# Differential attention beside an expert retrieval: other banks, other slots and a merged softmax in the attention steps

## The reference, cut to what matters

```python
def hybrid_mixer(x, ...):
    h = x @ w_in                                   # q, k, v, pooled input, gates
    q, k, v, p, g = split(h)
    a = softmax(q1 k1 * scale + bias) - lam * softmax(q2 k2 * scale + bias)   # 8 heads, causal, ALiBi
    o = rms_norm(a @ v, subln_g) * (1 - lam_init)
    attn_branch = o @ w_attn_proj
    pool_branch = (multiscale_pool(p) @ pool_w * pool_scale) @ w_pool_proj
    return (sigmoid(g_attn) * attn_branch + sigmoid(g_pool) * pool_branch) @ w_out
def peer_ffn(y, w_q, sub_keys, u, v):              # 8 heads, 16 experts each of 16384
    s = (y @ w_q) . sub_keys ; idx, gate = top-16 of the top-16 x top-16 sums, softmax
    act = gelu(u[idx] . y)
    return sum over 8 * 16 rows of gate * act * v[idx]
y = layer_norm(ALPHA * x + hybrid_mixer(x));  out = layer_norm(ALPHA * y + peer_ffn(y))
```

## Time and profile before

| what | value |
|---|---|
| time, median of 3 runs | 3320.99 us (3320.77 to 3330.28) |
| the profiled execution, its own time | 3328.37 us |
| its span | 3326.4 us |
| PE busy | 2798.8 us (84%) |
| DVE busy | 2475.0 us (74%) |
| ACT busy | 1162.4 us (35%) |
| POOL busy | 1324.7 us (40%) |
| DMA | 1244.97 MB, 374 GB/s over the span; the gathers are 1073.81 MB of it |

### The profile page before, as it was taken

The page is one execution under the profiler, slowest core; times in us unless marked ns, Lnnn a source line. Parts: engine busy times, 40 slices in busy tenths (PEclk is TensorE's granted clock), DMA queues, the critical chain, the costliest instruction groups (busy, mean ns, idle before and its releaser), DMA issues.

```text
span 3326.4 us, 30256 instructions
## 1 busy us (share of the span) xinstructions
PE 2798.8 (84%) x8368; PEld 1442.0 (43%) x8368; DVE 2475.0 (74%) x5989; ACT 1162.4 (35%) x3421; POOL 1324.7 (40%) x1248
## 2 busy tenths in 40 slices
PE   9999999999976799889988989867877777777776
PEld 7776565445433345444444544323433222222222
DVE  2316788896888778997799877888788676667664
ACT  2202555453122233445454522232323333333332
POOL 1101354554334343444454544344444444444432
PEclk9999999999998999999999999889989999999999
DMA  5635999999999999999999999999999999999997
GB/s 190 245 136 199 383 388 373 383 362 368 419 399 407 421 420 407 405 361 332 336 370 370 364 420 420 375 388 420 420 420 418 421 416 421 416 414 417 420 415 311
DMA packets 205223, 1244.97 MB, mean 374 GB/s; under 512 B 23680, under 2 KB 36992, under 8 KB 73600
## 3 DMA queue, kind: packets, MB, share of 16 engines
q0 software_dynamic: 147456, 1073.81, 79.8%
q1 hardware_dynamic: 56592, 169.11, 13.6%
q10 hardware_dynamic: 1008, 0.14, 0.0%
HBM read 1228.81 MB, written 14.16 MB: 374 GB/s over the span
## 4 chain that ended last, share of the span: by engine, by line
PE 41%; DMA 30%; DVE 18%; issue 6%; ACT 4%; POOL 1%; SPq 0%; POOLq 0%; DVEq 0%; ACTq 0%
DMA ring<-uv,idx 30%; PE r_o L1579 15%; PE w_ps L1373 14%; DVE ring L1306 8%; DVE z_e L1258 3%; PE w_ps L1421 2%; PE r_o L1550 1%; PE w_ps L1550 1%; PE w_ps L1516 1%; PE w_ps L1458 1%; PE w_ps L1493 1%; DVE e L1022 1%; POOL ring L706 1%; PE r_o L1493 1%; PE r_o L1516 1%
## 5 line engine op out<-in xcount | busy, mean ns | idle before, releaser
L706 POOL DMA_INDIRECT ring<-uv,idx x1024 | 1172.3, 1145 | 1722.9 <-PE r_o L1579 1231.0
L1579 PE MATMUL r_o<-ring,diag 128*128 128x512 f32 x2936 | 1445.6, 626 | 403.9 <-ACT diag L892 388.1
L1306 DVE CUSTOM_DVE_ANT_0 ring<-ring,ytok 128x1024 f32<-128x1024 f32 x768 | 937.1, 1221 | 234.1 <-DMA ring<-uv,idx 232.7
L1579 PEld LDWEIGHTS r_o<-ring,diag 128*128 128x128 f32 x2936 | 539.7, 195 | 1131.9 <-ACT diag L892 590.0
L879 ACT ACTIVATE gel<-dot 128x2 f32<-128x2 f32 x512 | 104.0, 203 | 1608.9 <-DVE dot L1306 1605.3
L1373 PE MATMUL w_ps<-x,w 128*128 128x384 f32 (+1 forms) x2112 | 655.4, 456 | 9.7 <-DMA x<-xT 5.9
L1373 PEld LDWEIGHTS w_ps<-x,w 128*128 128x128 f32 x2112 | 395.9, 192 | 230.0 <-issue 59.1
L1306 DVE CUSTOM_DVE_ANT_0 ring<-ring,zn 128x1024 f32<-128x1024 f32 x256 | 313.3, 1224 | 211.3 <-DMA ring<-uv,idx 211.3
L1258 DVE SCALAR_TENSOR_TENSOR z_e<-ring,coef,z_e 128x1024 f32<-128x1024 f32 x290 | 371.7, 1282 | 0.2 <-ACT coef L883 0.2
L892 ACT ACTIVATE diag<-ident,coef 128x128 f32<-128x128 f32 x734 | 262.8, 387 | 0.0
L883 ACT ACTIVATE coef<-gel,gate 128x1 f32<-128x1 f32 x1024 | 246.0, 287 | 16.8
(11 more groups left out here) (199 smaller groups left out, 2331.3 us busy)
## 6 DMA issues: line engine op xcount, KB each, us to landing
w<-w_in SPq DMA_DIRECT2D x132, 512.0 KB, 3.6
wq<-wq SPq DMA_DIRECT2D x46, 512.0 KB
wc<-w_branch SPq DMA_DIRECT2D x24, 768.0 KB, 8.4
ring<-uv,idx POOLq DMA_INDIRECT x1024
wo<-w_out SPq DMA_DIRECT2D x24, 512.0 KB, 10.7
xs<-x SPq DMA_DIRECT2D x8, 512.0 KB
out<-yn_e SPq DMA_DIRECT2D x8, 512.0 KB, 11.6
x<-xT SPq DMA_DIRECT2D x16, 192.0 KB, 4.0
```

The source lines that it names most:

```text
L706: nc.gpsimd.indirect_dma_start(out=ring[t % RING][:], out_offset=None, in_=a["uv"], in_offset=bass.IndirectOffsetOnAxis(ap=idx[:, slot:slo ...
L1306: nc.vector.tensor_tensor_reduce(ring[r][:, 0:D], ring[r][:, 0:D], y_of(n)[:], 1.0, 0.0, ALU.mult, ALU.add, dot[:, slot:slot + 1]).then_in ...
L1579: ins = nc.tensor.matmul(o_ps[n % 2][half][:], diag[(u - 1) % DIAGS][:], ring[t % RING][:, D + half * HALF:D + (half + 1) * HALF], start=s ...
```

## The change

* The values product (L1458) and the output turn (L1473) of groups 2 and 3 go to the two idle row-sum banks whenever their slot lies in 14 to 117 of a tile (from slot 78 on). Of group 3's 24 steps 20 lend the values' bank and 20 the output's; of group 2's steps 8 and 9. For these, the waits between output turns and scores, and between turns and `osb`, are gone; a tile's first sum waits for the last user.
* Group 3's step keeps its 7 slots, but its second chunk comes 3 slots after the first, and exponents, mix, turns, values and output come 1 to 3 slots later in it. Group 2's mix and what follows come 1 slot later. Everything behind group 3's attention comes 3 slots later, its scores too, so that VectorE adds 2 more rows.
* The mix is now e2 * ratio + e1 with ratio = -lambda * den1 / den2; the pass over the second softmax is gone. The first softmax's reciprocal is multiplied in where the values' product leaves PSUM (`osb`), for which the copy becomes a tensor_scalar.
* The exponent of the expert scores' softmax is put beside an attention exponent where one lies within 6 slots, and the copies of turned mixes stand ahead of exponents due in the same slot. `invert` and `share` come 4 slots later.

```diff
-DRAIN = (19, 23, 23)
+DRAIN = (19, 23, 26)
-DO_EXP = (3, 5, 5)
-DO_MIX = (5, 6, 6)
-DO_TURN = (8, 7, 7)
+DO_EXP = (3, 5, 6)
+DO_MIX = (5, 7, 8)
+DO_TURN = (8, 8, 10)
 TURN_LEN = (2, 2, 3)
-DO_ACROSS = (9, 8, 9)
-DO_VALUES = (11, 11, 13)
+DO_ACROSS = (9, 9, 11)
+DO_VALUES = (11, 12, 16)
-DO_OT = (22, 24, 25)
-BEHIND = (0, 4, 3)
+DO_OT = (22, 24, 27)
+SCORE_GAP = (2, 2, 3)
...
+def lent(slot):
+
+    return slot >= 78 and 14 <= slot % SLOTS < 118
...
+    def value_bank(g, k):
+        if values_lent(g, k):
+            return o_ps[((step_at(g, k) + DO_VALUES[g]) // SLOTS + 1) % 2][0]
         return o_ps[1][0] if g == 0 else ps[3]
...
+        def shares():
+            for g in range(1, RH * TT):
+                yield exponent_at(g)
+                exponent(g)
...
-                nc.vector.reciprocal(rden, den).then_inc(mix_step, 1)
-                dve.wait_ge(mix_step, 3 * m + 1)
-                nc.vector.tensor_scalar(c2, rden[:, 1:2], neglam, None, ALU.mult).then_inc(mix_step, 1)
-                dve.wait_ge(mix_step, 3 * m + 2)
-                nc.vector.tensor_scalar(both[:, 1, 0:n], both[:, 1, 0:n], c2, None, ALU.mult).then_inc(mix_step, 1)
-                dve.wait_ge(mix_step, 3 * m + 3)
+                nc.vector.reciprocal(rden[m % 4], den).then_inc(mix_step, 1)
+                dve.wait_ge(mix_step, 2 * m + 1)
+                nc.vector.tensor_scalar(ratio, rden[m % 4][:, 1:2], den[:, 0:1], neglam, ALU.mult,
+                                        ALU.mult).then_inc(mix_step, 1)
+                dve.wait_ge(mix_step, 2 * m + 2)
...
-                nc.vector.tensor_copy(osb_of(g, k)[:], value_bank(g)[:, 0:DV]).then_inc(o_copied, 1)
+                nc.vector.tensor_scalar(osb_of(g, k)[:], value_bank(g, k)[:, 0:DV], rden[m % 4][:, 0:1], None,
+                                        ALU.mult).then_inc(o_copied, 1)
...
-                    if c == 0 and g and k > BEHIND[g]:
-                        pe.wait_ge(o_ready, STEP0[g] + k - BEHIND[g])
+                    if c == 0 and output_behind(g, k):
+                        pe.wait_ge(o_ready, output_behind(g, k))
...
+                if output_lent(g, k):
+                    bank_free(step_at(g, k) + DO_OT[g])
+                elif g:
+                    pe.wait_ge(logit_done, scores_behind(g, k))
```

More of the change, by code:

```diff
@@ L86 @@
                (-23, -21, -8, -3, -1, 1, 3),
-               tuple(T_A[2] - 30 + 4 * i for i in range(7)))
+               tuple(T_A[2] - 32 + 4 * i for i in range(7)))
 LAST_UNITS = ((0, 2, 5, 7, 10, 12, 15, 17, 20),) + (tuple(range(0, 27, 3)),) * 2
-HEAD_UNITS = ((0, 3, 6, 9), (0, 3, 6, 11), (0, 5, 10, 16))
+HEAD_UNITS = ((0, 3, 6, 9), (0, 3, 6, 11), (0, 4, 8, 16))
 EARLY = T_A[0] + 30
@@ L124, in evacuated_at @@
 def evacuated_at(g, i):
+    if g == NG - 1 and i < UNITS - GATES_AT[-1]:
+        return unit_at(g, i) + 3
     return unit_at(g, i) + (2 if g else 3) + (4 if (g, i) == (1, 1) else 0)
@@ L238, in __call__, with turned_at, score_chunk_at, values_lent @@
         return self.nc.alloc_sbuf_tensor_at(name, shape, dtype, offset=int(BASE + kib * KB))
+def turned_at(g, i):
+    return unit_at(g, i) + (4, 3, 5)[g]
+def score_chunk_at(g, k, c):
+    return step_at(g, k) + SCORE_GAP[g] * c
+def lent(slot):
+    return slot >= 78 and 14 <= slot % SLOTS < 118
+def values_lent(g, k):
+    return g > 0 and lent(step_at(g, k) + DO_VALUES[g])
+def output_lent(g, k):
+    return g > 0 and lent(step_at(g, k) + DO_OT[g])
+def scores_behind(g, k):
+    at = step_at(g, k) + DO_OT[g]
+    return sum(2 for j in range(NSTEPS[g]) for c in range(len(chunks(g, j))) if score_chunk_at(g, j, c) <= at) + score_no(
+        g, 0, 0, 0)
+def output_behind(g, k):
+    at = [j for j in range(NSTEPS[g]) if not output_lent(g, j) and step_at(g, j) + DO_OT[g] < step_at(g, k)]
+    return STEP0[g] + at[-1] + 1 if g and at else 0
+def last_lent(n, is_lent, offset):
+    uses = [STEP0[g] + k for g in range(1, NG) for k in range(NSTEPS[g])
+            if is_lent(g, k) and (step_at(g, k) + offset[g]) // SLOTS == n]
+    return uses[-1] + 1 if uses else 0
+def exponent_at(g):
+    begin = TOPK * g - SEARCH_AHEAD + 14
+    steps = [step_at(j, k) + DO_EXP[j] for j in range(1, NG) for k in range(NSTEPS[j])]
+    return min([slot for slot in steps if begin <= slot < begin + 6], default=begin)
 def build(nc, ctx, a, ident, k_scr, v_scr, b_scr, y_scr, s_scr, out):
@@ L288, in build @@
     lam_t = at("lam_t", 63, [P, 2, DH])
[L290 to L293, removed]
+    st_a = at("st_a", 104, [P, 64])
+    mx, nmx, den, ssq, rstd_a = st_a[:, 0:4], st_a[:, 4:6], st_a[:, 6:8], st_a[:, 21:23], st_a[:, 23:25]
+    rden = [st_a[:, 32 + 2 * i:34 + 2 * i] for i in range(4)]
+    ms, mhalf_a, neglam, o_gain, le, lexp, ratio = (st_a[:, 25:27], st_a[:, 13:14], st_a[:, 14:15], st_a[:, 15:16],
                                                  st_a[:, 16:18], st_a[:, 18:20], st_a[:, 20:21])
@@ L857, in stage @@
         def stage(g):
-            return merged(units(g), pooling(g), exponents(g), turned_out(g), head_norm(g), first_norms(g), flipped(g),
-                          queries(g), scores_out(g))
+            return merged(units(g), pooling(g), turned_out(g), exponents(g), head_norm(g), first_norms(g),
+                          flipped(g), queries(g), scores_out(g))
         def exponent(g):
@@ L904, in _ @@
         act.sem_inc(yn_ready, 1)
-        advance = woven(all_stages(stage))
+        advance = woven(merged(all_stages(stage), shares()))
         advance(-4)
@@ L1064, in transposed @@
                     dve.wait_ge(q_unit, HP * g)
-                nc.vector.tensor_scalar(o_all[g][:, h, j * P:(j + 1) * P], out_bank(g)[:, 0:P], o_gain, None,
+                nc.vector.tensor_scalar(o_all[g][:, h, j * P:(j + 1) * P], out_bank(g, k)[:, 0:P], o_gain, None,
                                         ALU.mult).then_inc(o_ready, 1)
@@ L1442, in turns, with bank_free @@
                     ins.then_inc(a_turned, 1)
+        def bank_free(slot):
+            if slot < SLOTS:
+                pe.wait_ge(s_copied, HP)
+            else:
+                pe.wait_ge(joined, 2 * (slot // SLOTS))
         def values(g):
@@ L1577, in spread @@
                 pe.wait_ge(joined, 2 * (n - 2) + 2)
+            if slot == 0 and n:
+                if last_lent(n - 1, values_lent, DO_VALUES):
+                    pe.wait_ge(o_copied, last_lent(n - 1, values_lent, DO_VALUES))
+                if last_lent(n - 1, output_lent, DO_OT):
+                    pe.wait_ge(o_ready, last_lent(n - 1, output_lent, DO_OT))
             for half in range(2):
```

46 lines of the change are left out of this document (21 added, 25 removed).

## The result

The changed kernel takes 3288.31 us (median, 3283.2 to 3290.55), the kernel before, run beside it, 3324.3: ratio 0.9887, 95% interval 0.9868 to 0.9906, 38 us by the ratio.

A forecast was written before the change was run, and what follows sets the result against it. TensorE was taken to bound group 2's attention, hand-overs between engines group 3's, DMA the end. Group 3's 27 us and group 2's 5 made -32: 3296.4 us on the profiled scale, 3289 on the median's, range 3264 to 3320.

The forecast's parts named there:

- The copy aT: Group 3's window: TensorE waits 24.1 us for the copied mix; 20 us of it taken as gain.
- Logits: Group 3's window: TensorE waits 20.0 us for logits before scores; half, 10 us, taken, from one slot of margin.
- Output turns and `o_all`: TensorE's waits: 7 of 7.4 us before group 3's output turns, 5 of 11.0 us for `o_all` in group 2.
- Diagonals, at nothing: Group 3's window: TensorE waits 16.2 us for diagonals; between 0 and 16 us possible, nothing taken.
- VectorE's work: Group 3's window: 15.4 us of passes go, osb copies cost 1.3 us more; net 14 of 499.8 us.
- ScalarE at nothing: 26 table loads fewer, 33 to 60 us of ScalarE's time, counted as no gain.
- my sign had 27: Sign that the forecast is right: the gathers of slots 304 to 512 some 27 us shorter.
- The least of them is 29: Group 3's window: TensorE and VectorE each allow 37 us, DMA at most 29, taken 0.95 of 580 us.
- The rival of the diagonals: Group 3: closed waits come back at the diagonal; only about -5 us, 3316, chance 0.14.
- my sign for it: Sign that the forecast is wrong: TensorE waiting 40 us or more for diagonals in group 3.
- the rival of all holes: All TensorE holes close and its clock returns: -45 us in group 3, -12 in group 2, 3264, chance 0.10.
- Bunching of mix and logits, slower: Mix and next logits together on VectorE delay group 3's diagonals by 34 us; ends at +14, 3335, chance 0.09.

The follow-up runs named there:

- slots_only: Kernel before with only the new slots of groups 2 and 3, without lent banks, old mix and exponents: 3306.73 us, ratio 0.9948.
- own_exp: Changed kernel with the experts' softmax exponent at its own slot again and attention exponents ahead of aT copies due in the same slot: 3284.37 us, ratio 0.9878.
- old_g3: Changed kernel with group 3's old slots within a step and the old distance to the branches: 3304.57 us, ratio 0.9939.
- rest_only: Changed kernel with the mix, lent banks, both groups' slots and exponents undone, so only small shifts of units, `invert` and `share` stay: 3320.33 us, ratio 0.9987.
- mix_only: Kernel before with only the new mix (one pass fewer, osb scaled as it leaves PSUM): 3310.18 us, ratio 0.9953.
- lend_only: Kernel before with only the lent banks, old slots, mix and exponents: 3314.86 us, ratio 0.9966.
- thin_w: Changed kernel loading only an eighth of each w_in block from group 3's fourth unit on, so its output differs: 3282.67 us, ratio 0.9874.
- later_osb: Changed kernel with group 3's VectorE readings (osb, square, output write where the bank is lent) a slot later: 3285.26 us, ratio 0.9879.
- old_mix: Changed kernel with the second softmax scaled in a pass of its own again and osb a plain copy: 3295.75 us, ratio 0.9915.

## Why the prediction was right, and where not

The direction and the place were right: TensorE's holes in group 3's attention, closed by slots and banks. That 3289 stands beside 3288.31 is luck. The forecast took 32 us off a median of 3321; the kernel before, run beside the changed one, had 3324.3, and the gain was 36 us by the medians and 38 by the ratio. By its steps:

- *The copy aT, 20 of 24.1 us:* the wait went to nothing. Slots and order were not both needed for it: the later slots are enough (slots_only, own_exp), and with the old slots so are the copies' place and the shared table loads together (old_g3).
- *Logits, 10 of 20.0:* 17.7 went, but not for the reason given, the slot of margin for the second chunk. In rest_only, with the old slots, mix and banks, 15.6 of them are gone. The small shifts, for which the prediction has no term, did that (mix_only has none of this wait, lend_only 5.4); old_g3 with its 12.1 says that slots and shifts depend on each other. Which shift it was is open.
- *Output turns and `o_all`, 7 and 5:* the waits went from 7.4 to 0 and from 11.0 to 2.7. In group 3 a wait of 4.7 us for `o_all` is new. Lending as a whole was worth 7 to 14 us, 8 of them in group 2 when it is taken out, where I took 5.
- *Diagonals, at nothing:* this is the term that was most wrong. Of the 49 us of waits that went, 32 came back here (16.2 to 48.3). All idle time of TensorE in the window fell by 14.6 us, from 71.1 to 56.5, and not by 37.
- *VectorE's work:* 15.4 us less and some 60 ns a copy more, as costed. The mix was worth 9 to 11 us on the chip. That VectorE no longer waits for exponents (18 forecast, 18.8 measured) was partly eaten up by the wait for values, 11 us more.
- *ScalarE at nothing:* right, by own_exp.
- *The sum.* Group 3 was forecast at 27 and group 2 at 5; between the profiled executions they gave 35.5 and 10.1, 45 in all against 32 (38 by the ratio); the gathers of slots 304 to 512 took 32 us less, where my sign had 27. "The least of them is 29", the DMA engines' limit "if packets take as long as now", was no limit: 0.95 of the stage's 588.4 us is 559, and it took 552.9, at a share of 0.98 and 385 GB/s, so the packets took less time for nearly the same bytes. In thin_w the time stayed when loads were taken away.
- *The rival of the diagonals* named the wait that did come, and my sign for it, "40 us or more", was met without its outcome. TensorE's busy time for the same work also fell, from 508.9 to 494.0, as much as its idle time did. Of that, the values' matmuls account for 6.6 us (42.8 to 36.2: a mean of 304 ns before, 275 now) and the units for 5 (199.7 to 194.6), and both are mostly the clock: 17 us fewer at the low level in the stage. A part of the rival of all holes, that the clock comes back with them, came true. But busy time doesn't set the stage's time: thin_w has 41.0 us at the low level and 500.8 us busy, 4 more than the changed kernel, in 551.3 us.
- *Bunching of mix and logits, slower:* not seen. Of the 32 waits for diagonals (48.3 us) only three, 3.3 us in all, end within 9 us of the end of a mix.

What paces group 3 now isn't shown. Moving the waits (later_osb) does nothing, so it is not one hand-over. More work for VectorE cost 9 us (old_mix), and work moved from VectorE to TensorE cost 8 to 10, so neither engine alone is the one to relieve. The two together, handing over slot by slot, fit this, but no run separates how much each gives. The small shifts were not taken apart either.

## What to carry to other kernels

Where several engines hand work over in fixed order, write down for every wait how many places of the order lie between giver and taker. Here three waits with none or one, 52 us in all, went nearly to nothing, and slots and lending, which were meant for them, gave 20 us alone and 31 when taken out. So don't count closed waits as time: two thirds of them came back at another hand-over, the diagonals. Look at the whole idle and busy time of the engine instead. A busy share of DMA near 1 needn't be a bound where the engine that consumes the data hardly waits for it; taking away load tells it in one run. And run what is left when all named parts are undone: here it held most of a wait that was put down to another part.

## What the runs showed that I had not expected

- The DMA share is not a measure of how much more can be moved. It was 0.95 at 366 GB/s, 0.98 at 385, 0.95 at 357 with the thin loads, and 1.01 at 415 to 419 where DMA is the bound.
- 21 us of ScalarE's time in group 3's window, 16 table loads, had no price that could be measured, although every slot's diagonal comes from that engine.
- Every stretch of TensorE at half its clock in this stage (3.4 us in most cases) stood beside an idle time of 1.8 to 3.3 us. So the waits that were closed had a second price on the engine, the slower matmuls behind them; that the stage's time paid it is not shown.
